# An RWKV scan whose small products are spread over four corners of TensorE and two PSUM banks

## The reference, cut to what matters

```
def step(s, inp):
    r_t, w_t, k_t, v_t, kk_t, b_t = inp
    sa = jnp.einsum('bhvk,bhk->bhv', s, kk_t)
    s = s * w_t[:, :, None, :] - sa[..., None] * b_t[:, :, None, :] + v_t[..., None] * k_t[:, :, None, :]
    return s, jnp.einsum('bhvk,bhk->bhv', s, r_t)
```

## Time and profile before

| | |
|---|---|
| median of 3 runs | 3710.08 us (3709.4 to 3715.09) |
| time of the profiled execution | 3709.3 us |
| its span | 3707.5 us |
| mean granted clock of TensorE over the span, as a share of 2.4 GHz | 0.933 |
| TensorE busy (matmul) | 3239.4 us, 87% |
| VectorE busy | 1825.0 us, 49% |
| ScalarE busy | 1003.2 us, 27% |
| scan of 12 chunks, from its barrier to its last instruction | 462.2 to 771.4 us |

### The profile page before, as it was taken

The page is one execution under the profiler, slowest core; times in us unless marked ns, Lnnn a source line. Parts: engine busy times, 40 slices in busy tenths (PEclk is TensorE's granted clock), DMA queues, the critical chain, the costliest instruction groups (busy, mean ns, idle before and its releaser), DMA issues. The chain is left out here.

```text
span 3707.5 us, 66040 instructions
## 1 busy us (share of the span) xinstructions
PE 3239.4 (87%) x28824; PEld 2422.3 (65%) x28824; DVE 1825.0 (49%) x2962; ACT 1003.2 (27%) x1946; POOL 315.0 (8%) x196
## 2 busy tenths in 40 slices
PE   4996599968699999959797699997988998988997
PEld 1775278854588865547696288644877754877753
DVE  2036755532677720052376378504766723776822
ACT  2100344421222210022332233203535222525320
POOL 1231000000344400023000000000000000000000
PEclk6997799989899999979798899998989999999999
DMA  6560000011121211102000123221210221210221
GB/s 247 211 249 35 0 4 5 5 70 34 34 62 63 63 62 52 51 27 74 1 1 7 40 91 96 90 80 52 80 41 4 74 80 59 85 47 4 69 80 57
DMA packets 62628, 230.00 MB, mean 62 GB/s; under 512 B 7344, under 2 KB 7856, under 8 KB 62128
## 3 DMA queue, kind: packets, MB, share of 16 engines
q1 hardware_dynamic: 62384, 226.36, 18.5%
HBM read 224.24 MB, written 2.10 MB: 61 GB/s over the span
## 5 line engine op out<-in xcount | busy, mean ns | idle before, releaser
L367 PE MATMUL bank<-arena,ring 128*128 128x512 f32 (+1 forms) x1440 | 517.9, 523 | 7.0 <-POOLq L277 7.0
L367 PEld LDWEIGHTS bank<-arena,ring 128*128 128x128 f32 x1440 | 274.7, 191 | 247.8 <-issue 235.2
L427 DVE TENSOR_SCALAR arena<-bank 128x512 f32<-128x512 f32 (+1 forms) x16 | 9.3, 604 | 584.1 <-PE bank L420 584.1
L1404 DVE SCALAR_TENSOR_TENSOR arena<-arena,vec 128x512 f32<-128x512 f32 (+1 forms) x220 | 199.3, 922 | 25.5 <-DVE arena L1402 0.2
L333 PE MATMUL bank<-h_high_ffn,w_high_ffn 128*128 128x256 f32 x704 | 182.1, 341 | 29.6 <-POOL ring_low L311 29.6
L1982 DVE SCALAR_TENSOR_TENSOR x_all<-arena,vec,x_all 128x512 f32<-128x512 f32 x240 | 179.9, 750 | 10.4 <-ACT arena L2092 3.6
L333 PE MATMUL bank<-h_low,w_high_ffn 128*128 128x256 f32 x704 | 181.5, 339 | 0.0
L333 PE MATMUL bank<-h_high_ffn,ring_low 128*128 128x256 f32 x704 | 180.0, 336 | 0.0
L333 PE MATMUL bank<-h_high_d,w_high_d 128*128 128x512 f32 x384 | 157.5, 410 | 14.9 <-DVE h_low_d L2142 14.8
L333 PEld LDWEIGHTS bank<-h_high_ffn,w_high_ffn 128*128 128x128 f32 x704 | 132.8, 189 | 44.7 <-POOL ring_low L311 30.4
L1504 DVE SCALAR_TENSOR_TENSOR arena<-arena,vec 128x512 f32<-128x512 f32 x176 | 132.3, 752 | 53.7 <-ACT arena L1472 48.2
(11 more groups left out here) (475 smaller groups left out, 6797.6 us busy)
## 6 DMA issues: line engine op xcount, KB each, us to landing
arena<-in_ada_w_dram SPq DMA_DIRECT2D x96, 512.0 KB, 5.3
ring<-in_ffn_up_dram SPq DMA_DIRECT2D x88, 512.0 KB, 3.5
ring<-in_d_branch_dram SPq DMA_DIRECT2D x56, 512.0 KB, 3.5
ring<-in_ffn_down_dram SPq DMA_DIRECT2D x48, 512.0 KB, 3.5
ring<-in_d_in_dram SPq DMA_DIRECT2D x32, 512.0 KB, 3.4
ring<-in_ab_in_dram SPq DMA_DIRECT2D x19, 512.0 KB, 7.1
ring<-in_c_in_dram SPq DMA_DIRECT2D x17, 512.0 KB, 3.5
ring<-in_d_join_dram SPq DMA_DIRECT2D x16, 512.0 KB, 3.5
```

The lines of the kernel that those rows point to most:

```text
L367: ins = M.matmul(bank_of(tile % 2, seg), ring[slot][:, k * P:(k + 1) * P], rhs(done + k, seg), start=(done + k == 0), stop=(done + k == su ...
L427: ins = V.tensor_scalar(rt[:, seg[0]:seg[0] + seg[1]], psum[4 + (seg[0] == 0)][:, 0:seg[1]], scale, eps, ALU.mult, ALU.add)
L1404: ins = V.scalar_tensor_tensor(y, a, w(dy, dx), y, ALU.mult, ALU.add)
```

## The change

Quantities that lie by token (scores, turned keys, values, right side, solution, inverse) are now kept in the partition half given by the parity g = j % 2 of the head's pair, not by the head within the pair; the place along the row is 2h + q with q = j // 2. A product that goes from channels to tokens takes rows h and writes columns g, one that goes from tokens to channels takes rows g and writes columns h, and row half 0 writes bank 5, row half 1 bank 6 (`FILL`). So scores_b, scores_k, both tokens, the state part of the right side, and of the outputs and new state all but one product in five use four corners and two banks. The products from tokens to tokens (the values' part of the right side, `solve`) and from channels to channels (the state's part of the outputs) stay on the diagonal, in bank 7.

Since the two parts of the right side now lie in different banks, they are summed on DVE (`keep_right_side`), after ACT has copied the first (`keep_values_part`); the outputs are added to `yacc` in two steps. The two directions are no longer handled apart: right side, solve, outputs with new state are one filler each, and the fillers are placed anew. The wait for the outputs stands in `take_state` of direction 0 alone. `update` at level 0 and `couplings` write their pair and half indices swapped, with no more instructions than before. `grams` is written out and issues the same products in the same order. DVE's and ACT's orders change as the diff shows. The turning of the values in `lora_pe` goes to two banks and is copied in two pieces.

```
                 for j in range(4):
-                    for h in HALF:
-                        at = 256 * (n % 2) + 64 * j
-                        ins = M.matmul(psum[6 + pair % 2][h, at:at + 64], vT[h, j, n * RC:(n + 1) * RC], ident64[h],
-                                       start=True, stop=True)
+                    for h in range(2):
+                        at = 128 * (n % 2) + 64 * (j // 2)
+                        ins = M.matmul(psum[VALUES[pair % 2] + h][HALF[j % 2], at:at + 64],
+                                       vT[HALF[h], j, n * RC:(n + 1) * RC], ident64[HALF[h]], start=True, stop=True)
...
-            ins = S.activation(ring[slot][:, at:at + 512], psum[6 + pair % 2], ACT.Identity)
+            both = banks[:, 512 * VALUES[pair % 2]:512 * VALUES[pair % 2] + 1024].rearrange("p (h c) -> p h c", h=2)
+            for n in range(2):
+                ins = S.activation(ring[slot][:, at + 256 * n:at + 256 * n + 256].rearrange("p (h c) -> p h c", h=2),
+                                   both[:, :, 128 * n:128 * n + 128], ACT.Identity)
...
+    TWIN = (0, 2, 1, 3)
+    values_done, rhs_kept = signal("values_part_done"), signal("values_part_kept")
...
-    SCORES, TOKENS = (psum[6], psum[7], psum[7]), (psum[7], psum[6])
+    FILL = (psum[5], psum[6])
+    fill = banks[:, 2560:3584].rearrange("p (b c) -> p b c", b=2)
+
+    def heads_of_four():
+
+        for j in range(4):
+            for h in range(2):
+                yield j, j % 2, j // 2, h
...
         def scores_b(i):
             if i:
-                pe.wait_ge(tok_read, 2)
+                pe.wait_ge(tok_read)
             for d in range(2):
-                for j in range(4):
-                    for h in HALF:
-                        ins = M.matmul(SCORES[0][h, 256 * d + 64 * j:256 * d + 64 * j + 64], bT[d][h, j, chunk_at(d, i)],
-                                       keys(1, i, d, j, h), start=True, stop=True)
+                for j, g, q, h in heads_of_four():
+                    at = 128 * d + 64 * q
+                    ins = M.matmul(FILL[h][HALF[g], at:at + 64], bT[d][HALF[h], j, chunk_at(d, i)],
+                                   keys(1, i, d, j, HALF[h]), start=True, stop=True)
             ins.then_inc(scores_done.sem, 1)
...
+        def scores_k(i):
+            pe.wait_ge(scores_read)
+            for d in range(2):
                 for a in range(2):
-                    for h in HALF:
-                        at = 128 * j + 64 * a
-                        ins = M.matmul(SCORES[1 + d][h, at:at + 64], kdT[d][h, j, chunk_at(d, i)], keys(a, i, d, j, h),
-                                       start=True, stop=True)
+                    for j, g, q, h in heads_of_four():
+                        at = 256 * d + 128 * q + 64 * a
+                        ins = M.matmul(FILL[h][HALF[g], at:at + 64], kdT[d][HALF[h], j, chunk_at(d, i)],
+                                       keys(a, i, d, j, HALF[h]), start=True, stop=True)
             ins.then_inc(scores_done.sem, 1)
 
         def tokens(i, which):
-            if which == 0:
-                pe.wait_ge(scores_read)
-            elif i:
-                pe.wait_ge(state_ready)
+            pe.wait_ge(tok_read if which else rhs_ready)
...
+        def right_side(i):
+            pe.wait_ge(state_ready, 2)
+            if i == 0:
+                pe.wait_ge(scores_read, 2)
+            for d in range(2):
+                for c in range(4):
+                    for g in HALF:
+                        ins = M.matmul(psum[7][g, 256 * d + 64 * c:256 * d + 64 * c + 64], SC1[i % 2][d][g, c, 0, :],
+                                       VTOK[chunk_of(d, i)][g, c, :], start=True, stop=True)
+            ins.then_inc(values_done.sem, 1)
+            for d in range(2):
+                for q in range(2):
+                    at = 128 * d + 64 * q
+                    for g in range(2):
+                        for h in range(2):
+                            ins = M.matmul(FILL[h][HALF[g], at:at + 64], KR0[i % 2][HALF[h], d, 2 * q + g, :],
+                                           ST[d][HALF[h], 2 * q + g, :], start=True, stop=True)
             ins.then_inc(rhs_done.sem, 1)
 
-        def solve(i, d):
-            pe.wait_ge(sa_ready if d else rhs_ready)
-            for j in range(4):
-                for h in HALF:
-                    ins = M.matmul(psum[5][h, 256 * d + 64 * j:256 * d + 64 * j + 64], XT[i % 2][h, j, d, :],
-                                   RS[h, d, j, :], start=True, stop=True)
+        def solve(i):
+            for d in range(2):
+                for c in range(4):
+                    for g in HALF:
+                        at = 256 * d + 64 * c
+                        ins = M.matmul(psum[7][g, at:at + 64], XT[i % 2][g, TWIN[c], d, :], RS[g, d, c, :],
+                                       start=True, stop=True)
             ins.then_inc(sa_done.sem, 1)
...
+        def outputs(i):
+            if i + 1 < NCH:
+                pe.wait_ge(scores_read, 2)
+            else:
+                pe.wait_ge(tok_read)
+            pe.wait_ge(sa_ready)
...
+                    y = lambda g, h: FILL[g][HALF[h], 256 * d + 128 + 64 * q:256 * d + 192 + 64 * q]
+                    st = lambda g, h: FILL[g][HALF[h], 256 * d + 64 * q:256 * d + 64 * q + 64]
+                    for g in range(2):
+                        for h in range(2):
+                            j = 2 * q + g
+                            M.matmul(psum[7][HALF[h], 256 * d + 64 * j:256 * d + 64 * j + 64], GT[d][HALF[h], j, chunk_at(d, i)],
+                                     ST[d][HALF[h], j, :], start=True, stop=True)
+                    for out, lhs, rhs, first, last in (
+                            (y, SC1[i % 2][d][:, :, 1, :], VTOK[n], True, False),
+                            (y, SC0[i % 2][:, d], RS[:, d], False, True),
+                            (st, kdT[d][:, :, chunk_at(d, i)], VTOK[n], True, False),
+                            (st, bT[d][:, :, chunk_at(d, i)], RS[:, d], False, True)):
+                        for g in range(2):
+                            for h in range(2):
+                                ins = M.matmul(out(g, h), lhs[HALF[g], 2 * h + q, :], rhs[HALF[g], 2 * h + q, :],
+                                               start=first, stop=last)
...
@@ -1045,11 +1066,8 @@
             if i:
                 step(i - 1, 1, 5)
                 tokens(i - 1, 1)
-                right_side(i - 1, 0)
             pe.wait_ge(prepared, 2)
             grams(i, 0)
-            if i:
-                right_side(i - 1, 1)
             for lv in range(1, 6):
                 forward(i, 0, lv)
                 if lv == 1:
@@ -1057,38 +1075,24 @@
                     scores_b(i)
                 else:
                     step(i, 1, lv - 1)
-                if i and lv == 2:
-                    solve(i - 1, 1)
+                if lv == 2:
+                    scores_k(i)
                 if i and lv == 3:
-                    outputs(i - 1, 0)
-                if lv == 4:
-                    scores_k(i, 1)
-                if i and lv == 5:
-                    new_state(i - 1, 1)
+                    outputs(i - 1)
+                if lv == 5:
+                    tokens(i, 0)
                 forward(i, 1, lv)
                 step(i, 0, lv)
                 if i and lv == 1:
-                    solve(i - 1, 0)
-                if lv == 2:
-                    scores_k(i, 0)
-                if i and lv == 3:
-                    new_state(i - 1, 0)
-                if i and lv == 4:
-                    outputs(i - 1, 1)
-                if lv == 5:
-                    tokens(i, 0)
+                    solve(i - 1)
+                if lv == 4:
+                    right_side(i)
...
-        for d in range(2):
-            right_side(NCH - 1, d)
         pe.wait_ge(xt_last, 2)
-        pe.wait_ge(tok_read, 2)
-        for d in range(2):
-            solve(NCH - 1, d)
-        for d in range(2):
-            outputs(NCH - 1, d)
-            new_state(NCH - 1, d)
+        solve(NCH - 1)
+        outputs(NCH - 1)
...
+        def keep_values_part():
+            act.wait_ge(values_done)
+            S.activation(RS.rearrange("p d c t -> p (d c t)"), psum[7], ACT.Identity).then_inc(rhs_kept.sem, 1)
+
+        def keep_solved():
+            act.wait_ge(sa_done)
+            S.activation(RS.rearrange("p d c t -> p (d c t)"), psum[7], ACT.Identity).then_inc(sa_ready.sem, 1)
 
...
         for i in range(NCH):
             if i:
                 keep_tokens(i - 1, 1)
-                for d in range(2):
-                    keep_five(rhs_done, rhs_ready, d)
             for lv in range(1, 6):
                 for s in range(2):
+                    if s and lv == 5:
+                        keep_tokens(i, 0)
                     keep_turned(i, s)
                     keep_half(s)
-                    if i and lv == 2 - s:
-                        keep_five(sa_done, sa_ready, 1 - s)
```

(55 more changed lines are left out.)

91 lines of the change are left out of this document (30 added, 61 removed).

## The result

The changed kernel takes 3735.57 us (median of 5 runs, 3732.85 to 3742.76), the kernel before 3711.74 on the same chip: ratio 1.0066, 95% interval 1.0052 to 1.0081, 23.8 us more. The profiled execution took 3737.25, 28 more than that of before.

The account below looks back on a forecast made before the run. PE was taken as full, bound by fillers beyond the 0.63 us its update chain hides. Terms -1.9 - 1.1 + 1.0 + 0.1 - 4.2 gave 3703.2 us; eleven clock falls, +18.7, made 3721.9, range 3699 to 3740.

Parts of the forecast that it names:

- the mechanism of hole and clock: In the scan's chunks, PE idle some 2 us makes the granted clock fall to 1.2 GHz for some 3.4 us.
- the walk: Chunks 1 to 10, timed half-level by half-level without a clock change: 24.63 us a chunk against 24.53, +1.0 in all.
- Values' turns: In `lora_pe`, products on four corners let the last copy end earlier: -1.9 us, bounds 0 and -2.1.
- Chunk 0: The scan's first chunk: -1.1 us from its half-levels at an unchanged clock, and one clock fall costing 1.7.
- the hole of B2: Level 2, half-level with turn(1), chunks 0 to 10: PE idle 2.04 us, DVE's update queued behind `prepare_keys`; half-level 3.11.
- Chunks 1 to 10, the clock: One clock fall a chunk, mostly in outputs or right side, 1.7 us each; part of +18.7 for eleven falls.
- Chunk 11 and the end of the scan: Last chunk: no stall from exponentials but longer other half-levels, +0.1 us; last tokens to last DVE op 8.4 for 12.6, -4.2.
- (a): Rival: the clock holds throughout the scan; 3703.2 us, give or take 4; chance 0.24.
- (c): Rival: level 2's wait for exponentials is absent, its update 1.48 us earlier, the clock holds; 3687 us; chance 0.10.
- (d): Rival: the new groups miss four corners' pace, 160 products at 58 ns, 4.6 us a chunk more; 3755; chance 0.04.
- Rival (b): The clock falls twice a chunk or stays low longer, 3.4 us a chunk; 3740 us; chance 0.14.
- B3 with A4: Level 3's half-level with turn(1) and level 4's with turn(0), no filler: PE 1.15 us idle, 1.0 busy, 0.85 idle.

Follow-up runs that it names:

- the fourth experiment: The kernel before with the change of the values' turns alone, the scan's operands then lying in another order: 3707.02 us, ratio 0.9984.

## Why the prediction came out as it did

Direction, the mechanism of hole and clock, and the walk were right; a third loss, the waits for instructions, had no term; the size was 13.7 us short (3721.9 against 3735.57), inside the range of 3699 to 3740 and outside the forecast's own 3710 to 3730. Term by term, in the profiled executions:

- **Values' turns, -1.9.** The scan started 4.05 earlier. The part reckoned is there (VectorE's scans start at 409.77 for 411.32, 8.50 after the first product for 10.29). The rest is the clock in the `bonus` products: two groups take 1.53 instead of 2.90 here, one did in the fourth experiment.
- **Chunk 0, -1.1 and one fall of 1.7.** It took 28.0 for 23.4, +4.7, at a mean clock of 0.64 for 0.89. This is the worst mis-sized term. The clock comes up only 9.3 us after the first turn, where it took 4.5, and behind the hole of B2 it is down again for 10.2 us, where one fall of 1.7 was reckoned. The second part is the hole's: with the queues mended, PE's program being the same, the clock came up as late but stayed, and the chunk took 24.1. With spare products it took 25.7.
- **Chunks 1 to 10, the walk, +1.0.** Ten times the clean chunk would be +6.5. Of its 0.65 over 24.53, 0.1 was forecast, 0.3 is the half-level with the wait by issue, and 0.25 is small errors of the walk.
- **Chunks 1 to 10, the clock, +17.** Nine of ten chunks had a fall. What they lost beyond the clean chunk is 18.3 us, of which about 5 are idle time by issue (the waits above without the 1.10 that lies in chunk 11), so the falls cost some 13: nine, of 3.4 us at 1.2 GHz each and one of 6.8, which cost about 1.4 us each and 2.4, where the prediction has ten of 1.7.
- **The missing term.** Those 5 us by issue, and more once the clock holds: 11 in the kernel with spare products, 22 in the one with the fillers spread. The prediction took 14.5 ns an instruction as what any group on corners costs, from the `step` of 16. Groups of 64 and 128 keep it as long as their instructions are there, and are broken by waits when they are not.
- **Chunk 11 and the end of the scan, +0.1 and -4.2.** From chunk 11's first update to the last operation 36.0 for 35.4. Chunk 11 took 25.8 from its first turn to the end of its tokens, for 21.8: its right side ran at a mean clock of 0.60 (+1.3), and waits by issue of 1.10 in its outputs and of 0.4 in `scores_k` fell into it. From there to the last operation it was 9.7 us, for the 12.6 of before and the 8.4 that were forecast; the last outputs hold a wait by issue of 1.20. So the 4 us gained were lost.

Sum: -4.05 + 4.7 + 24.8 + 0.6 = 26.0; the later stages differ by 2 more, which is about what two executions of one kernel differ by.

Of the rivals, (a) fell with the clock of 0.94, (c) with the 2.03 us, (d) with the pace of the corners. Rival (b), two falls a chunk, named nearly the right time for a wrong reason: most chunks had one fall, and the rest came from issue and chunk 0. Forecasting one fall per chunk was right as a count (nine in ten), and its place too, the outputs or the right side. For its cause the prediction had named both the hole of B2 and the idle time of B3 with A4, without choosing. The hole alone would have been wrong: with it at 0.56 us in every chunk six of ten still fell, and in the kernel before a hole of 1.1 us from the same queue order cost no clock. That the total came within 13.7 us (15.4 in the profiled executions) is in part luck: the walk was 5.5 short, the missing term 5, chunk 0 and the end of the scan over 4 each, while the falls cost 4 less and the values' turns gave 2 more.

On the Trainium skill (TensorE: Matmul & The Clock Gate, "Why this matters for your kernels"), whose advice is to keep gaps under about 3 us: holes of 2.03 us and less cost the clock here, with only short work around them, and filling them restored it. The traces contradict the advice as a guarantee.

What stays open: how far ahead of its use a transfer of instructions is begun, and so how long a dense run may be before PE waits; and why the clock falls in one chunk and not in the next with the same holes. Whether a version with fewer, larger products would keep the gain was not tried.

## What to carry to other kernels

Halving the time of filler work pays only where the filler was longer than the chain it hides: walk the chain slot by slot, and spread the fillers over all slots before making any of them faster. An engine that is no longer full can pay twice, in idle time and in granted clock, and the mean clock of a chunk tells which chunk to read the walk from. Short dense instructions pay a third time when they are used up faster than they are brought in, so look at the waits that no engine ends. And look at how the work behind another engine's wait is queued: an operation of the next chunk ahead of an update cost 9 to 12 us by itself, in the kernel before, though it cost PE's clock nothing there.

## What the runs showed of the hardware

- 64x64 products on four corners cost 14.5 ns an instruction in groups of 16 to 64, but dense runs of them bring idle times of 0.2 to 1.6 us that no semaphore explains, at full clock, 6 us over eleven chunks of the changed kernel and 22 with the fillers spread. With two of the groups on the diagonal (29 ns each) there were 0.4.
- All 164 of these idle times end 1.2 to 1.6 us after a 16 KB transfer of instructions landed. There are 6.5 such transfers a chunk, in the kernel before as well, which has no such idle time.
- The granted clock fell in nine of ten chunks with PE busy 80% of the time and no hole over 2.03 us in them, and its mean was 0.93, with falls in six of ten, where PE waited for another engine 1.2 us at most (and for its instructions 1.6); with PE kept busy in two holes of the chunk it was 1.00 in all ten.
